# Prompt attention: logits in single-pass products of stacked high and low parts, and the causal mask added in the same kind

## What is computed

```python
def sb_block(q_blk, q_start, k, v, bias):
    valid = k_pos[None, :] < q_pos[:, None]
    z = jnp.einsum('bqhd,bkhd->bhqk', q_blk, k) + bias[None, :, None, None]
    lneg = jnp.where(valid, jax.nn.log_sigmoid(-z), 0.0)
    suffix = lax.cumsum(lneg, axis=3, reverse=True) - lneg
    w = jnp.where(valid, jnp.exp(jax.nn.log_sigmoid(z) + suffix), 0.0)
    return jnp.einsum('bhqk,bkhd->bqhd', w, v)
```

## Time and profile before

| what | value |
|---|---|
| median of 3 runs | 3538.48 us (3536.65 to 3539.49) |
| profiled execution | 3538.79 us |
| its span, first to last instruction | 3537.2 us |
| TensorE busy | 3277.4 us, 93% |
| VectorE, ScalarE, GpSimd busy | 46%, 39%, 26% |
| mean granted TensorE clock | 0.959 |
| bytes moved by transfers | 439.01 MB |

### The profile page before, as it was taken

The page is one execution under the profiler, slowest core; times in us unless marked ns, Lnnn a source line. Parts: engine busy times, 40 slices in busy tenths (PEclk is TensorE's granted clock), DMA queues, the critical chain, the costliest instruction groups (busy, mean ns, idle before and its releaser), DMA issues. The chain is left out here.

```text
span 3537.2 us, 49773 instructions
## 1 busy us (share of the span) xinstructions
PE 3277.4 (93%) x17836; PEld 2402.0 (68%) x17836; DVE 1617.4 (46%) x1930; ACT 1391.9 (39%) x2281; POOL 915.2 (26%) x917
## 2 busy tenths in 40 slices
PE   7999999678699699999999799999999999499998
PEld 6999999344388599999999344444444444366665
DVE  5111121566533321111122488888888787334442
ACT  5111111444411211111111477778778786234442
POOL 0000000455401000000000366666666565000000
PEclk9999999788899899999999699999999999799999
DMA  4222121433444422212221632232323200799995
GB/s 145 72 72 70 59 64 49 153 128 123 164 137 166 156 96 72 67 66 65 72 67 54 175 100 84 70 92 84 108 49 105 63 28 12 272 340 369 349 344 204
DMA packets 223746, 439.01 MB, mean 124 GB/s; under 512 B 22997, under 2 KB 130202, under 8 KB 211514
## 3 DMA queue, kind: packets, MB, share of 16 engines
q1 hardware_dynamic: 203626, 334.04, 28.8%
q0 software_dynamic: 19952, 102.77, 8.2%
HBM read 312.76 MB, written 124.00 MB: 123 GB/s over the span
## 5 line engine op out<-in xcount | busy, mean ns | idle before, releaser
L1656 POOL TENSOR_TENSOR att_w<-att_w,att_rest 128x1023 f32<-128x1023 f32 (+7 forms) x384 | 613.2, 1599 | 375.3 <-DVE att_rest L1621 372.2
L455 PE MATMUL projb_acc<-projb_x_hi,projb_w_hi 128*128 128x416 f32 x1280 | 452.8, 354 | 27.0 <-DVE projb_x_lo L445 27.0
L455 PE MATMUL projb_acc<-projb_x_hi,projb_w_lo 128*128 128x416 f32 x1280 | 450.8, 352 | 0.0
L455 PE MATMUL projb_acc<-projb_x_lo,projb_w_hi 128*128 128x416 f32 x1280 | 450.3, 352 | 0.0
L1528 PE MATMUL att_z<-att_k,att_q 64*128 64x512 f32 (+3 forms) x1280 | 403.4, 590 | 1.8 <-ACT att_w L1579 1.7
L1571 ACT ACTIVATE att_rest<-att_z,att_bias 128x1024 f32<-128x1024 f32 (+7 forms) x384 | 333.0, 867 | 135.6 <-PE att_z L1528 113.9
L1492 PEld LDWEIGHTS att_wT_acc<-const_ident,att_w 128*128 128x128 f32 x2176 | 232.7, 141 | 216.2 <-issue 116.1
L1621 DVE TENSOR_TENSOR_SCAN att_rest<-att_rest,att_zero 128x128 f32<-128x128 f32 (+7 forms) x256 | 358.6, 1406 | 21.9 <-ACT att_rest L1571 21.2
L292 PE MATMUL proja_acc<-proja_x_hi,proja_w_hi 128*128 128x416 f32 x1000 | 354.2, 354 | 0.8 <-DVE proja_x_lo L265 0.7
L292 PE MATMUL proja_acc<-proja_x_hi,proja_w_lo 128*128 128x416 f32 x1000 | 352.4, 352 | 0.0
L292 PE MATMUL proja_acc<-proja_x_lo,proja_w_hi 128*128 128x416 f32 x1000 | 350.3, 350 | 0.0
(11 more groups left out here) (236 smaller groups left out, 4726.7 us busy)
## 6 DMA issues: line engine op xcount, KB each, us to landing
smp_k_pages<-in_cache_k SPq DMA_DIRECT2D x128, 512.0 KB, 6.5
smp_v_pages<-in_cache_v SPq DMA_DIRECT2D x128, 512.0 KB, 6.8
proj_b<-projb_out POOLq DMA_DIRECT2D x32, 1040.0 KB, 4.7
proj_a<-proja_out POOLq DMA_DIRECT2D x24, 1040.0 KB, 4.5
att_q<-proj_b SPq DMA_DIRECT2D x64, 256.0 KB, 4.1
att_k<-proj_b SPq DMA_DIRECT2D x14, 1024.0 KB, 13.3
proja_w_raw<-in_w_in_a SPq DMA_DIRECT2D x24, 512.0 KB, 4.1
gla_vgT<-proj_a SPq DMA_DIRECT2D x24, 512.0 KB, 5.8
```

Source lines behind the costliest of these rows:

```text
L455: mm = pe.matmul(acc[:, q, 0:size], w[:, b, k, :], x[:, k, at:at + size], start=(k == 0 and w is w_hi and x is x_hi), stop=(k == KD - 1 an ...
L1656: pool.tensor_tensor(these, these, passed[:, 1:size], ALU.mult).then_inc(w_made, 1)
```

## The change

In `project`, the 16 blocks of keys and queries are of a new kind "parts". For them ScalarE makes a second, rounded copy of each span of the accumulator (into `slab`, free by then), VectorE subtracts it from the accumulator for the low part, and GpSimd stores both to new tensors `kq_hi` and `kq_lo`, beside the float32 block. In `prompt_attention`, `q_hi` and `q_lo` each hold the queries' part twice, and `k2` holds the high part of the keys in one half of the partitions and the low part in the other, changing sides every 512 keys. A first product over all 128 rows gives q_hi times (k_hi + k_lo); a second over the 64 rows that hold k_hi gives q_lo times k_hi. The fourth term, low by low, is dropped, so the computation is the reference's to within that rounding. The mask and the identity are fp32r too. To make room, the turned keys and the rows to be turned are kept for 512 tokens at a time.

```diff
@@ def build_constants
+            pool.wait_ge(c.consts_ready, 3)
+            pool.tensor_copy(c.ident_r[:, :], c.ident[:, :])
+            pool.tensor_copy(c.diag_mask_r[:, :], c.diag_mask[:, :])
...
@@ def project: scalar
                     act.activation(out[:, b, at:at + size], acc[:, q, 0:size],
-                                   ACT.Sigmoid if gate else ACT.Copy).then_inc(copied, 1)
+                                   ACT.Sigmoid if kind == "gate" else ACT.Copy).then_inc(copied, 1)
+                    if kind == "parts":
+                        if q == 0 and from_tile(no, 1):
+                            act.wait_ge(parts_stored, no * 32)
+                        act.activation(high(at, size), acc[:, q, 0:size], ACT.Copy).then_inc(high_made, 1)
...
@@ def project: vector
+                    elif kind == "parts":
+                        dve.wait_ge(high_made, no * n_spans + (q + 1))
+                        dve.tensor_tensor(low(at, size), acc[:, q, 0:size], high(at, size).bitcast(F32),
+                                          ALU.subtract).then_inc(low_made, 1)
...
@@ def project: tensor
+                    if last_kind == "parts":
+                        pe.wait_ge(low_made, last_no * n_spans + (q + 1))
...
@@ def project: gpsimd
+                if kind == "parts":
+                    pool.wait_ge(low_made, no * n_spans + n_spans)
+                    pool.dma_start(parts[0][ds(no * P, P), :], high(0, SEQ).bitcast(F32)).then_inc(parts_stored, 16)
+                    pool.dma_start(parts[1][ds(no * P, P), :], low(0, SEQ).bitcast(F32)).then_inc(parts_stored, 16)
...
@@ def prompt_attention: sync
+            def load_k_span(pair, u, sem):
+                for half in range(2):
+                    sp.dma_start(k2[half * HD:(half + 1) * HD, pair % 2, :, u * BANK:(u + 1) * BANK],
+                                 head_rows(0 if u % 2 == half else 1, k_parts + pair * P)[:, :, u * BANK:(u + 1) * BANK]
+                                 ).then_inc(sem, 16)
...
+                for part, dst in enumerate((q_hi, q_lo)):
+                    for half in range(2):
+                        sp.dma_start(dst[half * HD:(half + 1) * HD, g, :, :],
+                                     head_rows(part, q_parts + pair * P)[:, :, g * BANK:(g + 1) * BANK]
+                                     ).then_inc(in_q[g], 16)
...
@@ def prompt_attention: tensor, logits
                 if not carried:
-                    pe.matmul(z_ps[:, n % 2, size - P:size], c.ident_bf[:, :], c.diag_mask[:, :], start=True,
+                    pe.matmul(z_ps[:, n % 2, size - P:size], c.ident_r[:, :], c.diag_mask_r[:, :], start=True,
                               stop=False, skip_group_check=True)
-                for half, at in enumerate(range(0, size, BANK)):
-                    rows, end = slice(half * HD, (half + 1) * HD), min(at + BANK, size)
-                    pe.matmul(z_ps[:, n % 2, at:end], q2[rows, t // 4, h, (t % 4) * P:(t % 4 + 1) * P],
-                              k2[rows, pair % 2, h, lo + at:lo + end], start=carried or end < size, stop=True,
-                              skip_group_check=True).then_inc(z_made, 1)
+                tile = slice((t % 4) * P, (t % 4 + 1) * P)
+                ends = [(at, min(at + BANK, size)) for at in range(0, size, BANK)]
+                for at, end in ends:
+                    pe.matmul(z_ps[:, n % 2, at:end], q_hi[:, t // 4, h, tile].bitcast(F32R),
+                              k2[:, pair % 2, h, lo + at:lo + end].bitcast(F32R),
+                              start=carried or end < size, stop=False, skip_group_check=True)
+                for half, (at, end) in enumerate(ends):
+                    rows = slice(half * HD, (half + 1) * HD)
+                    pe.matmul(z_ps[:, n % 2, at:end], q_lo[rows, t // 4, h, tile].bitcast(F32R),
+                              k2[rows, pair % 2, h, lo + at:lo + end].bitcast(F32R),
+                              start=False, stop=True, skip_group_check=True).then_inc(z_made, 1)
...
@@ def prompt_attention: scalar, turn
-                    if m == 0 and pair:
-                        act.wait_ge(kv_stored, 32 * pair)
+                    if m >= 2 or pair:
+                        act.wait_ge(k_stored[m % 2], 16 * (2 * pair + m // 2))
```

More of the change, by code:

```diff
@@ L338, in _, with project @@
             pool.wait_ge(stored[1], 16 * (blocks // 2))
-def project(nc, c, name, xnT, jobs, first_gate):
+def project(nc, c, name, xnT, jobs, parts):
     with ExitStack() as stack:
@@ L363, in project @@
         n_spans = len(spans)
[L364 to L383 removed]
+        n_blocks = sum(count for _, _, kinds, _, _ in jobs for _, count in kinds)
@@ new lines, in project, with high, low @@
+        n_parts = sum(count for _, _, kinds, _, _ in jobs for kind, count in kinds if kind == "parts")
+        def high(at, size):
+            return slab[:, 0, at:at + size].bitcast(F32R)
+        def low(at, size):
+            return slab[:, 1, at:at + size].bitcast(F32R)
+        def over_blocks(engine, step, skip_first=False):
+            last, done, used = (None, 0), 0, {"parts": 0, "plain": 0, "gate": 0}
+            for j, (_, _, kinds, _, _) in enumerate(jobs):
+                jb = 0
+                for kind, count in kinds:
+                    no = used[kind]
+                    if done or not skip_first:
+                        step(j, jb, done, done // 2, 0, (kind, no), last)
+                    step(j, jb + 1, done + 1, done // 2, 1, (kind, no + 1), (kind, no))
+                    with engine.Fori(1, count // 2) as i:
+                        for b in range(2):
+                            step(j, i * 2 + (jb + b), i * 2 + (done + b), i + done // 2, b, (kind, i * 2 + (no + b)),
+                                 (kind, i * 2 + (no + b - 1)))
+                    used[kind], last = no + count, (kind, no + count - 1)
+                    jb, done = jb + count, done + count
@@ L405, in _, with step @@
                 act.activation(x_hi[:, k, :], slab[:, k % 2, :], ACT.Copy).then_inc(x_hi_made, 1)
-            def step(j, jb, n, i, b, width, gate, follows_gate):
+            def step(j, jb, n, i, b, this, last):
+                kind, no = this
                 for q, (at, size) in enumerate(spans):
@@ L447, in _, with products @@
             over_blocks(dve, step, skip_first=True)
-            multiply_gate(n_blocks - 1, 1)
+            finish(n_blocks - 1, 1, "gate", 0)
         @block.tensor
         def _(pe):
-            def products(b, width, k, q):
+            def products(b, k, q):
                 at, size = spans[q]
@@ L480, in _, with step @@
         def _(pool):
-            def step(j, jb, n, i, b, width, gate, follows_gate):
-                if gate:
-                    pool.wait_ge(gate_made, (n - first_gate) * n_spans + n_spans)
+            def step(j, jb, n, i, b, this, last):
+                kind, no = this
+                if kind == "gate":
+                    pool.wait_ge(gate_made, no * n_spans + n_spans)
                 else:
@@ L1437, in load_first_k @@
             def load_first_k(u):
-                for half in range(2):
-                    sp.dma_start(k2[half * HD:(half + 1) * HD, 0, :, u * BANK:(u + 1) * BANK],
-                                 projT[k_rows:k_rows + P, u * BANK:(u + 1) * BANK].rearrange("(h p) n -> p h n", p=HD)
-                                 ).then_inc(in_first_k[u], 16)
+                load_k_span(0, u, in_first_k[u])
             load_q(0, 0)
@@ L1465, in _ @@
                             load_k(pair + 2)
-                elif kind == "turn" and x[0] == 3:
-                    for e, (dst, src) in enumerate(((k_out, k_tok), (v_out, v_tok[:, pair % 2, :, :]))):
-                        sp.wait_ge(copied[e], turn_end[pair])
-                        sp.dma_start(dst.rearrange("(t p) n -> p t n", p=P)[:, :, pair * P:(pair + 1) * P],
-                                     src[:, :, :]).then_inc(kv_stored, 16)
-                    if pair + 1 < PAIRS:
-                        load_raw(pair + 1)
+                elif kind == "turn":
+                    m, = x
+                    for e in range(2):
+                        sp.wait_ge(copied[e], ring_no[(kind, pair, m)] + 1)
+                    if m < 2:
+                        load_raw(pair, m + 2)
+                    elif pair + 1 < PAIRS:
+                        load_raw(pair + 1, m - 2)
+                    sp.dma_start(k_out.rearrange("(t p) n -> p t n", p=P)[:, 4 * m:4 * m + 4, pair * P:(pair + 1) * P],
+                                 k_tok[:, m % 2, :, :]).then_inc(k_stored[m % 2], 16)
+                    if m == 3:
+                        sp.dma_start(v_out.rearrange("(t p) n -> p t n", p=P)[:, :, pair * P:(pair + 1) * P],
+                                     v_tok[:, pair % 2, :, :]).then_inc(v_stored, 16)
                 elif kind == "gate":
```

134 lines of the change are left out of this document (60 added, 74 removed).

## The result

| | before | with the change |
|---|---|---|
| median | 3538.48 us (3 runs) | 3498.56 us (4 runs) |
| its runs | 3536.65 to 3539.49 | 3494.02 to 3504.69 |
| profiled execution | 3538.79 us | 3504.69 us |

A fourth run of the kernel before, 3788.67 us, was disturbed and is left out. The ratio is 0.9889, with an interval of 0.9870 to 0.9909: some 40 us faster, where 47 were forecast. The profiled execution of the change is its slowest, 6 us above the median. So stages are compared one by one here, and whole times by their medians.

A forecast was written before the change was run, and what follows sets the result against it. TensorE was taken to bound the projection and "first", "above" and nearly all of "middle", VectorE to be fuller in "below" and "rest". 52 us for eight pairs less 2.3 and 2.6 in pair 0 gave 47 off 3538.8: 3492, range 3474 to 3528.

The forecast's parts named there:

- the likeliest case: Whole kernel: the forecast itself, 3492 us, on its own 3474 to 3515, given 71%.
- The price of a step: Logit steps in prompt attention: unmasked 0.15 us less, masked 0.04 to 0.33 less by number of keys.
- From the first q_hi product to the values 1.00 us: Unmasked step of prompt attention: sign of being right, 1.00 us after the change for 1.15 before the change.
- Six full beats at TensorE's pace: Unmasked steps of a pair: six of 16 in full beats give 0.15 us each, staying above VectorE's 2.84.
- The two turn beats about as much: Phase "below": its two turn beats give about 0.15 us each too, 1.2 a pair with the six full beats.
- GpSimd's two extra stores: zero: Projection: the two extra 1 MB stores cost nothing, ScalarE running late by up to 12 us with 18 of slack.
- I take that phase's own 2.3 us as lost: "First" of pair 0: its 2.3 us gain lost to rows queued behind 2 MB of keys; bounds 6 gained, 15 lost.
- A clock below 1.00 after pair 0: Prompt attention after pair 0: a granted clock below 1.00 (2.4 GHz) would show the forecast wrong.
- Low parts in sequence: Rival, logit steps: q_lo products in the two halves don't run beside each other; 2.2 us less a pair, 3526; 10%.
- The clock: Rival, "first" of every pair: a quieter array gets the lower clock, 14 us more a pair, 3607; 5%.
- Slow restarts between kinds: Rival, 38 TensorE-paced steps a pair: single-pass products restart 0.15 us slower between other kinds, 3538; 5%.
- A thinner cover: Rival: pair 0's transfers cost 15, unmasked steps give nothing, "middle" and "above" half; 3526 to 3535; 9%.

The follow-up runs named there:

- the new mask alone: The kernel before with its mask as fp32r and nothing else of the change; one run, 3546.74 us beside 3533.92.
- the loads spread out: The changed kernel with pair 0's late loads spread: queries of group 1 after turn 3, group 3 and pair 1's keys at pair 1's turns; 3496.03 us, ratio 0.9884.
- all that helped: Changed kernel with bf16 mask, whole-array low part under 1024 keys, values copied by ScalarE, loads spread, parts stored by SyncE; 3444.04 us, ratio 0.9749 to the kernel before.

## Why the prediction was right

The time, 3498.56, lies in the range and 6.6 above the forecast, and the likeliest case was the one that came. In the traces, where stages can be compared, the end of prompt attention comes 38.5 us earlier (3006.24 to 2967.73), and by terms:

| term | forecast | measured |
|---|---|---|
| projection | 0 | -1.1 |
| its last product to attention's first | +2.6 | +4.6 |
| pair 0 | -4.2 | -1.6 |
| pairs 1 to 6 | -39 | -36.4 |
| pair 7 and the tail | -6.5 | -4.1 |

- **The price of a step** held to 0.02 us in sum: 1.91 for 1.93, 0.62 for 0.62, 0.97 for 0.97. In part this is luck, for two errors cancel. "From the first q_hi product to the values 1.00 us" was to be the sign, and it is 1.07 (2617.80 to 2618.87); the eight transposes ahead take 0.84 and not 0.93. The 0.93 was read in front of a bf16 mask, and 0.08 of it is that mask's kind (the new mask alone). So 1.02 less 0.93 wasn't the change of shape alone. What makes up for it is q_hi: its two products and the change of shape take 0.65, priced at 0.56. Over the whole array they take 0.55, priced at 0.47, so 0.08 of the miss is q_hi's own, which was priced by its columns alone, and half rows behind it cost 0.10, near the 0.09.
- **Which beats get it.** Scan to scan, six beats of pair 5 took 3.09 before: the last of "first" and of "above", and two each in "below" and "rest" (2687.08 to 2690.00 is 2.92 now). "Six full beats at TensorE's pace" was right: they are 0.16 to 0.21 shorter, 1.0 us in sum for 0.9. "The two turn beats about as much" was wrong: they gave nothing, for 0.3. The first is the ring through VectorE above, 4.10 before too, and the rows of "below" would have shown it; the run with the values on ScalarE bears it out. Without the two unmasked beats at their ends, "first", "middle" and "above" together are 5.0 shorter for 5.3. Those two are why these phases (2.34 and 3.04 less for 2.3 and 3.0) look nearer to the forecast than the masked steps in them are. In sum a pair gives 6.07 for 6.5, so 0.43 is missing, 2.6 in pairs 1 to 6.
- **The start.** Of 4.6 us, 1.9 are the extra issues ahead of the first logits (forecast 2.6) and 2.6 the drain at the end of GpSimd's block. "GpSimd's two extra stores: zero" was right for TensorE inside the projection and wrong at its end. Storing the parts from SyncE takes just that away.
- **Pair 0.** "I take that phase's own 2.3 us as lost" was too little: "first" of pair 0 grew from 36.43 to 41.06, 4.6 lost rather than 2.3 not gained. The mechanism (rows behind the keys) was named and its bound of 15 held; the block was 4 MB, as the queries' loads count too. The run with the loads spread out shows it. TensorE waiting for `att_raw` had been named as a sign of being wrong; it came, for 7.00 us. "Below" of pair 0 gave 2.7 back (27.21 to 24.48), where the other pairs give 0.35; that was not in the sum. In part it is the clock, whose mean in that phase was 0.86 before and 0.93 now.
- **Pair 7** has a "middle" of 23.37 in this trace and of 21.6 to 21.8 in seven of the nine experiments with the new attention. The two rows below show why: for 3.4 us the granted clock was 0.50, the lower level, behind 3.8 us in which TensorE was busy for 2.30 and waited 1.50 for VectorE's gated output. "A clock below 1.00 after pair 0" was a sign of being wrong; it came, for 3.4 us. Where the same wait of 1.5 was followed by 1.00 (the parts stored by SyncE), the phase took 21.78; with 6.8 us at 0.50 (the loads spread out), 24.81. So 1.6 of these 23.37 are the clock and not the steps. The three traces with the old attention have no such fall, and TensorE waits 1.07 at that place; three of the ten with the new one have it. Whether the change makes it more likely stays open.

```profile
2876.00:2879.80 3.80, 2.30 (x17) 1.37 (x16) 3.80 (x6) 2.06 (x4) 3.56 (x3) 1.00 0.00 0
2879.80:2883.20 3.40, 3.40 (x15) 2.14 (x14) 3.18 (x3) 1.64 (x3) 2.58 (x2) 0.50 0.48 157
```

- **The rivals.** Low parts in sequence: against it two q_lo in 0.42, as long as one, and the run with whole-array low parts in all steps. The clock: 1.00 in all five phases of pair 5. It stayed at 0.50 until 2012.8 in pair 0 (until 2006.3 before) and came back for 3.4 us in pair 7, so that rival has a small place. Slow restarts between kinds: none in sum, at steps that hold to 0.02. A thinner cover: part of it came (pair 0's transfers, the turn beats), at a fraction of its price; "middle" and "above" arrived nearly whole.
- **The mask** in the new kind was priced at 0.09 behind a values product, and is 0.08 (bf16 mask in the change) to 0.10 (new mask alone). The Trainium skill ("TensorE: Matmul & The Clock Gate", weight-path perf modes) says that 16-bit weights load faster than float32 ones. These two runs agree with it, though they show the mask's whole price and not its load by itself. This part of the change is a loss of 5.0 us.

What stays open: why q_hi ahead of half the rows costs 0.1 more and q_lo in half the rows up to 0.2 more, and whether it is the load of the weights or the switch that holds; the whole-array run takes both away at once. The projection's 1.1 lie in the wait for its first operands (27.0 to 25.9), which varies from 25.9 to 29.4 in all these traces.

## What to carry to other kernels

Price a product by its passes and, apart from that, by its fixed part: here 0.2 to 0.3 us of a short step came from using half the rows, and giving that up (and computing a term that nobody needs) gained 24 to 28 us on top of the change's 40. Before taking the price of a switch from two rows, see that they differ in nothing else: here one of them had a change of kind in it. Before counting a shorter step as a gain, read for each beat which ring closes it, scan to scan; a beat whose ring runs through another engine keeps its length. When loads are doubled, look at the queue's order at the start of the stage, where rows that are needed soon stand behind rows that are not.

## What was not expected of the hardware

- GpSimd's drain at the end of a block of the program was longer where it had issued more transfers in it: 2.11 us with 25, 2.67 with 32, 5.28 with 64, on the path. It isn't the number alone: another stage's block with 34 had 0.88, one with none 3.11, and that of prompt attention with 2 had 17.06. What the parts stored by SyncE show is that 32 transfers fewer take 2.6 off in this block.
- The granted clock in "first" of pair 0 was 0.50 over the 10 us from 1985 to 1995, in which TensorE was busy for 10.00, and 0.52 in the phase when 7 us of its waits were gone. It was 0.73 there in the kernel with all that helped, whose "first" of pair 0 took 28.32. The same steps have 1.00 in all later pairs. No run here tells what decides it.
